# Tile-by-tile queries in the head of a two-layer decoder trunk, and the first expert choice in two groups of heads

## What is computed

```python
q = (hc @ w_query).reshape(T, PEER_HEADS, 2, PEER_DK)
s = jnp.einsum('thpd,phnd->thpn', q, sub_keys)
top_s, top_i = lax.top_k(s, K_SUB)
cand = top_s[:, :, 0, :, None] + top_s[:, :, 1, None, :]
best_s, best_c = lax.top_k(cand.reshape(T, PEER_HEADS, K_SUB * K_SUB), PEER_TOPK)
expert = i1 * N_KEYS + i2          # i1, i2: top_i at best_c
gate = softmax(best_s)
act = gelu(einsum('thkd,td->thk', u_tab[expert], hc))
x += einsum('thk,thkd->td', gate * act, v_tab[expert])
```

## Time and profile before

| | |
|---|---|
| runs | 3590.6, 3592.1, 3597.78 us; median 3592.1 |
| the profiled execution: span from its first to its last instruction | 3593.4 us (the page gives no other time of that execution) |
| PE busy | 2864.7 us, 80% |
| DVE busy | 2512.9 us, 70% |
| ACT busy | 1388.5 us, 39% |
| POOL busy | 1310.8 us, 36% |
| transfers | 1296.92 MB, mean 361 GB/s |
| mean granted TensorE clock | 0.900 |
| first expert row issued | at 463.60 us |

### The profile page before, as it was taken

The page is one execution under the profiler, slowest core; times in us unless marked ns, Lnnn a source line. Parts: engine busy times, 40 slices in busy tenths (PEclk is TensorE's granted clock), DMA queues, the critical chain, the costliest instruction groups (busy, mean ns, idle before and its releaser), DMA issues. The chain is left out here.

```text
span 3593.4 us, 28215 instructions
## 1 busy us (share of the span) xinstructions
PE 2864.7 (80%) x8084; PEld 1470.3 (41%) x8084; DVE 2512.9 (70%) x5180; ACT 1388.5 (39%) x3442; POOL 1310.8 (36%) x1033
## 2 busy tenths in 40 slices
PE   8899787778989778777988778878998786556556
PEld 4554635435436334433436334535445432112112
DVE  1411577787767979787667969787767977777775
ACT  2321225456433344456423344457433242223222
POOL 0000033345333344445433333345433334554552
PEclk9989898889999989889999989989999897778777
DMA  4224289899999999999999999899999999999996
GB/s 159 104 82 164 100 364 373 345 415 420 421 421 371 402 391 404 383 407 421 421 413 378 378 391 389 349 405 421 421 421 386 367 378 422 421 422 396 421 422 269
DMA packets 182971, 1296.92 MB, mean 361 GB/s; under 512 B 20384, under 2 KB 21920, under 8 KB 28192
## 3 DMA queue, kind: packets, MB, share of 16 engines
q0 software_dynamic: 147456, 1073.81, 72.8%
q1 hardware_dynamic: 35360, 221.31, 15.6%
HBM read 1292.94 MB, written 2.10 MB: 360 GB/s over the span
## 5 line engine op out<-in xcount | busy, mean ns | idle before, releaser
L590 POOL DMA_INDIRECT ring<-in_uv,experts x1024 | 1308.3, 1278 | 2235.9 <-DVE x L1310 928.6
L1434 PE MATMUL ps_sum<-ring,diag 128*128 128x512 f32 x2060 | 1172.7, 712 | 567.5 <-ACT diag L855 566.4
L1301 DVE SCALAR_TENSOR_TENSOR ring<-ring,h_ffn 128x1024 f32<-128x1024 f32 x1024 | 1236.1, 1220 | 298.3 <-DMA ring<-in_uv,experts 291.4
L1434 PEld LDWEIGHTS ps_sum<-ring,diag 128*128 128x128 f32 x2060 | 423.6, 220 | 1198.7 <-ACT diag L855 820.3
L1310 DVE SCALAR_TENSOR_TENSOR x<-ring,weight,x 128x1024 f32<-128x1024 f32 x509 | 652.6, 1282 | 164.0 <-ACT weight L859 163.7
L853 ACT ACTIVATE diag<-ident,dots 128x128 f32<-128x128 f32 x515 | 205.8, 400 | 725.1 <-DVE ring L1301 714.9
L857 ACT ACTIVATE dots<-dots 128x1 f32<-128x1 f32 x509 | 101.8, 200 | 686.0 <-DVE ring L1301 684.5
L1572 PE MATMUL ps_act<-area_h,wt 128*128 128x256 f32 x1536 | 348.3, 385 | 2.6 <-ACT area_h L606 2.6
L1700 PE MATMUL ps_act<-wt,area_h 128*128 128x512 f32 x768 | 338.3, 594 | 10.9 <-DMA wt<-in_weights 10.9
L1572 PEld LDWEIGHTS ps_act<-area_h,wt 128*128 128x128 f32 x1536 | 294.5, 193 | 61.4 <-issue 17.9
L1496 PE MATMUL ps_act<-wt,area_h 128*128 128x512 f32 (+1 forms) x704 | 306.3, 595 | 4.2 <-ACT area_h L606 4.2
(11 more groups left out here) (193 smaller groups left out, 2178.4 us busy)
## 6 DMA issues: line engine op xcount, KB each, us to landing
wt<-in_weights SPq DMA_DIRECT2D x182, 1024.0 KB, 9.1
ring<-in_uv,experts POOLq DMA_INDIRECT x1024, 13.4
wt<-in_weights SPq DMA_DIRECT2D x8, 832.0 KB, 9.0
wt<-in_weights SPq DMA_DIRECT2D x11, 512.0 KB, 8.2
wt<-in_weights SPq DMA_DIRECT2D x4, 768.0 KB, 8.8
x<-in_x SPq DMA_DIRECT2D x4, 512.0 KB, 5.2
area_y<-in_keys SPq DMA_DIRECT2D x4, 512.0 KB, 11.5
area_f<-in_keys SPq DMA_DIRECT2D x4, 512.0 KB, 14.9
```

The source lines that it names most:

```text
L590: pool.indirect_dma_start(ring[:, row.slot, :], None, a[f"uv{row.step // 2}"][:, :], bass.IndirectOffsetOnAxis(ap=experts[:, row.step % 2, ...
L1301: dve.scalar_tensor_tensor(u, u, 1.0, h_ffn[:, row.tile, :], ALU.mult, ALU.mult, accum_out=dots[:, row.j:row.j + 1]).then_inc(dots_ready, 1)
L1434: ins = pe.matmul(ps_sum[:, b, :], diag[:, row.pe_before % DIAGS, :], ring[:, row.slot, D + b * 512:D + (b + 1) * 512], start=row.pe_first ...
```

## The change

In the head, the queries are computed tile by tile. All eight query weight tiles are loaded into the eight slots of `ring`, which hold no rows yet, each with a semaphore of its own (`held`), and stay there for tile 1. `tile_query` computes one head for 128 tokens (`tile_scores` and `tile_rank` likewise). The choice of tile 0 is done in two groups of four heads (`topk_half`): the first group in the head, the second in step 0. GpSimd starts with row 0 when the first group's experts are there, and waits for the rest at row 64. Each of its first eight rows waits also until tile 1's query of that slot's head is through PE. The second group, the queries, scores and ranks of tile 1, and `x_norm` and `qkv` of step 1 are now stages of step 0, and the choice of tile 1 is spread between the stages of `x_norm` and the projection. The ffn row, the head's first gate and the scratch of the first choices lie in `area_kv` instead of `area_f`, `ring` and `area_y`. The diff shows ScalarE's `tile_scores` and PE's `tile_query`. Scores lie in `area_e` by head, all eight heads of one tile. Steps 1 to 3 keep their order. The four lines behind `TOPK_HALF_OPS` belong to `ROWS_IN`, `PE_PART`, `TICKS` and `ROWS_FIRST`.

```diff
+    "tile_query": (1, 0, 0, 0), "tile_scores": (1, 0, 0, 0), "tile_rank": (0, 0, 0, 10),
+TOPK_HALF_OPS = [3, 8, 8, 12, 4, 4, 4]
...
+    "tail_norm": 8, "tail_out": 6, "tile_query": 0, "tile_scores": 0, "tile_rank": 2.4, "topk_half": 1.6,
+           "out": 0, "query": 0.5, "scores": 0.5, "rank": 0.5, "topk": 1, "topk_half": 1, "taps": 1, "diff_sq": 1, "diff_norm": 1,
+         "out": 4, "query": 2, "tile_query": 2, "tail_out": 3}
+              "mla_qk", "mla_rope", "mix_turn", "rank", "tile_rank", "topk", "topk_half")
...
+    if stage[0] == "tile_rank" and stage[2] == 0:
+        return (0, 0, 0, 0, 0, 0, 0, 1)[stage[3]]
...
+def half_choice(g):
+    return [("topk_half", 0, 0, part, g) for part in range(len(TOPK_HALF_OPS))]
+
+def first_tile():
+    out = [("tile_query", 0, 0, 0)]
+    for i in range(1, 5):
+        out += [("tile_query", 0, 0, i), ("tile_scores", 0, 0, i - 1), ("tile_rank", 0, 0, i - 1)]
+    more = [[("tile_query", 0, 0, i), ("tile_scores", 0, 0, i - 1)] for i in range(5, HEADS)] + [[("tile_scores", 0, 0, HEADS - 1)]]
+    for i, part in enumerate(half_choice(0)):
+        out += [part] + (more[i] if i < len(more) else [])
+    return out
+
+def second_tile():
+    more = [[("tile_query", 0, 1, 0)]]
+    more += [[("tile_query", 0, 1, i), ("tile_scores", 0, 1, i - 1)] for i in range(1, HEADS)] + [[("tile_scores", 0, 1, HEADS - 1)]]
+    out = []
+    for st in [("tile_rank", 0, 0, i) for i in range(4, HEADS)] + half_choice(1):
+        out += [st] + (more.pop(0) if more else [])
+    return out + [("tile_rank", 0, 1, i) for i in range(HEADS)]
...
     if step == 0:
-        out += choice(0, 1)
+        out += second_tile()
...
-        for i in range(HEADS + 1):
+        for i in range(HEADS + 1 if d else 0):
...
-        out += choice(d, 0)
+        out += choice(d, 0) if d else first_tile()
...
-    if step < 1:
-        ahead = [("x_norm", 1)] + [("qkv", 1, n) for n in range(3)]
-        out = [st for st in out if st not in ahead]
-        if step < 0:
-            last = [st for st in out if st[0] == "topk"][-4:]
-            out = behind(out, [(("rank", 0, HEADS - 1), ahead[:1]), (last[0], ahead[1:2]), (last[3], ahead[2:])])
+    if step == 0:
+        ahead = [("x_norm", 1), ("qkv", 1, 0), ("qkv", 1, 1), ("diff_sq", 1), ("diff_norm", 1), ("qkv", 1, 2), ("diff_turn", 1, 0)]
+        second = choice(0, 1)
+        out = behind(out, [(("tile_rank", 0, 1, HEADS - 1), second[:1])] + [(place, [part]) for place, part in zip(ahead, second[1:])])
...
-                    load(0, NT_PLE + 4, DENSE_TILES[4:-HEADS])
+                    sp.dma_start(ffn_rows[0], a["ffn_rows"][0]).then_inc(row_loaded, 16)
+                    first = len(DENSE_TILES) - HEADS - 2 * HEADS
+                    load(0, NT_PLE + 4, DENSE_TILES[4:first])
+                    for i in range(HEADS):
+                        load(0, NT_PLE + first + 2 * i, DENSE_TILES[first + 2 * i:first + 2 * i + 2])
+                        sp.dma_start(ring[:, i, :], a["weights"][0, NT_PLE + NT_DENSE - HEADS + i, :, :]).then_inc(held[i], 16)
...
-                if row.j == 0:
+                if number == 0:
+                    pool.wait_ge(half_ready, 1)
+                elif row.j == 0 or number == ROWS // 2:
                     pool.wait_ge(experts_ready, row.tiles_before + 1)
-                if number >= RING:
+                if number < RING:
+                    pool.wait_ge(for_act, WHERE[("tile_query", 0, 1, number)].evacs + 1)
...
+            def tile_scores(at, d, t, i):
+                act.wait_ge(act_ops, at.act)
+                if t:
+                    act.wait_ge(dve_ops, WHERE[("tile_rank", d, 0, i)].dve + 10)
...
+            def tile_query(at, d, t, i):
+                hT_ready(WHERE[("tile_query", d, 0, 0)])
+                pe.wait_ge(held[i], 16)
+                w, b = ring[:, i, :].rearrange("p (k n) -> p k n", k=KT), act_bank()
+                for c in range(2):
+                    for k in range(KT):
+                        ins = pe.matmul(b[:, c * P:(c + 1) * P], w[:, k, c * P:(c + 1) * P], hT[:, k, t * P:(t + 1) * P],
+                                        start=(k == 0), stop=(k == KT - 1))
+                    if c:
+                        to_act(ins)
+                    tick()
```

More of the change, by code:

```diff
@@ L81, in counts @@
         return (0, part == len(TOPK_OPS) - 1, 0, TOPK_OPS[part])
+    if stage[0] == "topk_half":
+        part = stage[3]
+        return (0, part == len(TOPK_OPS) - 1, 0, TOPK_HALF_OPS[part])
     return COUNTS[stage[0]]
@@ L473, in trunk @@
         keys_loaded = sem("keys_loaded")
+        held = [sem(f"held{i}") for i in range(HEADS)]
         consts_made = sem("consts_made")
@@ L674, in x_norm @@
                     act.wait_ge(x_loaded[d], 16 * 2)
-                norm(at, d, "g_mix", ring[:, 1, 0:D] if d == 1 else squares[:, 0:D])
+                norm(at, d, "g_mix")
             def qkv(at, d, n):
@@ L840, in _ @@
                          branch_more=nothing, mix_turn=mix_turn,
-                         out=out, rows=nothing, tail_norm=tail_norm, tail_out=tail_out, ffn_norm=ffn_norm, query=query, scores=scores, rank=nothing, topk=topk, topk_late=topk)
+                         out=out, rows=nothing, tail_norm=tail_norm, tail_out=tail_out, ffn_norm=ffn_norm, query=query, scores=scores, rank=nothing, topk=topk, topk_late=topk,
+                         tile_query=tile_query, tile_scores=tile_scores, tile_rank=nothing, topk_half=topk)
             rows = Rows()
@@ L1193, in rank, with topk @@
                         link()
-            def topk(at, d, t, part):
-                sums = cand.rearrange("p (h i j) -> p h i j", h=HEADS, i=TOPK)
+            def topk(at, d, t, part, g=None):
+                hs = heads_in(g)
+                heads = range(hs.start, hs.stop)
+                n_heads, js = len(heads), slice(hs.start * TOPK, hs.stop * TOPK)
+                part_i, exps = part_is[d][:, :, js], exps_at[d][:, hs, :]
+                sums = cand.rearrange("p (h i j) -> p h i j", h=HEADS, i=TOPK)[:, hs, :, :]
                 lists = cand.rearrange("p (h c) -> p h c", h=HEADS)[:, :, 0:CANDS]
@@ L1213, in topk @@
+                    op(dve.scalar_tensor_tensor(top_f[:, hs, :, :].rearrange("p h c k -> p (h c) k"),
+                                                iota[:, :].unsqueeze(1).to_broadcast([P, 2 * n_heads, TOPK]), 128.0,
+                                                top_i[:, t, 2 * hs.start:2 * hs.stop, :], ALU.mult, ALU.add))
                 elif part == 1:
-                    for h in range(HEADS):
+                    for h in heads:
                         op(dve.max(best_v[:, h, 0:8], lists[:, h, :]))
@@ L1279, in _ @@
                          branch_first=branch, branch_more=branch,
-                         mix_turn=nothing, out=out, rows=nothing, tail_norm=tail_norm, tail_out=tail_out, ffn_norm=ffn_norm, query=nothing, scores=nothing, rank=rank, topk=topk, topk_late=topk)
+                         mix_turn=nothing, out=out, rows=nothing, tail_norm=tail_norm, tail_out=tail_out, ffn_norm=ffn_norm, query=nothing, scores=nothing, rank=rank, topk=topk, topk_late=topk,
+                         tile_query=nothing, tile_scores=nothing, tile_rank=tile_rank, topk_half=topk)
             rows = Rows()
@@ L1769, in _ @@
                          branch_more=branch, mix_turn=mix_turn,
-                         out=out, rows=nothing, tail_norm=tail_norm, tail_out=tail_out, ffn_norm=ffn_norm, query=query, scores=scores, rank=nothing, topk=nothing, topk_late=nothing)
+                         out=out, rows=nothing, tail_norm=tail_norm, tail_out=tail_out, ffn_norm=ffn_norm, query=query, scores=scores, rank=nothing, topk=nothing, topk_late=nothing,
+                         tile_query=tile_query, tile_scores=tile_scores, tile_rank=nothing, topk_half=nothing)
             pe.wait_ge(consts_loaded, 16 * N_CONSTS)
```

104 lines of the change are left out of this document (61 added, 43 removed).

## The result

The changed kernel takes 3614.07 us (median of 4 runs), the kernel before 3591.35 in the same comparison; the ratio is 1.0063, 95% interval 1.005 to 1.0077. The profiled execution spans 3609.9 us against 3593.4. The time lies above the stated range.

What follows compares the result with a forecast made beforehand. Row transfers at 421 GB/s were taken to bound all behind the head; 62.6 us earlier start less 5, 30 and 13 gave 14.6, taken as 15: 3577 us. Range 3552 to 3600, the forecast's own 3565 to 3587.

Steps and rivals of the forecast that it cites:

- Row 0 and the small matmuls: Head: 128-column query matmuls take 0.111 us each, so row 0 is issued at about 401 instead of 463.6, 62.6 us earlier.
- The slower rival: Head queries: small matmuls wait for their weights, 0.19 for 0.111 us, giving 3600 us or more; chance 0.14.
- The loop: First eight rows of step 0: PE alternates tile 1's queries with rows, 30 us newly empty, from 12 to 40.
- Fewer rows in the rest of the step: Later stages of step 0 get 0.948 instead of 1.158 rows a unit, 18% fewer; costs 13 us, 7 to 27.
- the gates: Gates of step 0: with 29 instead of 35 rows PE becomes the bound, and some 7 us open.
- all other stretches: Stretches of step 0 where transfers already pause keep their chains and lose rows: 6 us, between 0 and 20.
- The sum: Whole kernel: 62.6 - 5 - 30 - 13 = 14.6 us gained, taken as 15.
- the 5 us of weights: Start of step 0: two more of step 1's projection weight tiles fall behind the first row, costing 5 us.
- My check from step 2: Step 0 judged by step 2's 821.0 us: 836 to 851 us from row 0, a gain of 10 to 25.
- The engine-bound rival: PE's or VectorE's work sets step 0's length: gain -19 to +11, around 3592 us, no change; chance 0.17.

Runs made afterwards that it cites:

- thinner_before: The kernel before with 9.99 instead of 3 for each part of tile 1's choice in step 0 in the planner's table; 3628.9 us, 1.0099.
- groups_only: The kernel before with only tile 0's choice split in two groups of four heads, rows behind the first group; 3587.65 us, 0.9981.
- whole_choice_thicker: whole_choice_thick with 0.6 for a rank and 0.6 for a part of tile 1's choice, fewer rows ahead of the squares; 3570.35 us, 0.9938.
- whole_choice_thick: whole_choice_in_head with 1.2 for a rank, 1.5 for a part of tile 1's choice, and ScalarE's exponential moved earlier; 3558.39 us, 3562.63 in a second set.
- rows_behind_queries: The changed kernel with no row worked off before tile 1's last query, those rows given to tile 1's ranks; 3577.86 us, 0.9968.
- queries_first_thick: rows_behind_queries with fewer rows early: 1.2 instead of 3.5 for a rank, 1.5 instead of 3 for a part of tile 1's choice; 3590.3 us, 0.9996.
- share_shift: The kernel before with the running sum that deals rows to PE or VectorE started at 0.5 instead of 0.0; 3585.39 us, 0.9982.
- whole_choice_in_head: The changed kernel without the two groups: all of tile 0's choice in the head, tile 1's queries beside it on PE; 3577.45 us, 0.9967.
- thick_late: The changed kernel with fewer rows early in step 0: 1.0 for a rank of tile 1, 1.5 for a part of its choice; 3601.52 us, 1.0027.
- projection_behind: The kernel before with only the norm and projection of step 1 moved from the head into step 0; 3583.18 us, 0.9982.

## Why the prediction was wrong

1. **Row 0 and the small matmuls: right.** 402.27 for 401; a query of 128 columns takes 3.57 us, 0.112 us an instruction over runs of 32, for 0.111. The slower rival, whose place was here, fell. The Trainium skill (TensorE: Matmul & The Clock Gate, Back-to-back issue gap) gives 81 ns for a matmul of 128 columns in a stream of load and matmul pairs and 56 ns by itself; the factor of 1.45 estimated from that does not show in this trace: 0.112 us against 0.108, half of 0.216.

2. **The loop: right in mechanism, too small in size.** Rows 3 to 7 were forecast for 412, 424, 430, 437.5 and 451, and came at 413, 427, 434, 443 and 459. The term was 30 us newly empty; the first 60 us at 129 GB/s have 60 x (1 - 129/421) = 41.6 us of empty time, and the first 60 us before, at 412 GB/s, had 1.3. So 40 us are new, the upper bound of the term (12 to 40). Each row came 1 to 8 us later than I had put it.

3. **"Fewer rows in the rest of the step", 13 us with 7 to 27: this is the step that failed most.** Behind the first 60 us the step has 125.5 - 41.6 = 84 us of empty time, 48 before: 36 more, beyond the upper bound. The direction was right, the gates too (11 us for my 7). I had put 6 us on all other stretches. By their rates they opened by 7 us (squares to gates), 14 us (behind the gates) and 3 us (before the squares). My error was to look for stages that turn engine-bound in the gates alone. The reason shows in thinner_before, where one number of the table was changed: 22 rows less between squares and gate save 350.3 - 313.7 = 37 us of the 55 that their transfers take, six rows less in the gates save 1.5 of 15, and behind them 17 MB less (41 us at 421 GB/s) save 26.5 us. In the gates it is plain that PE sets the pace. For the other two stretches, where no engine is busy all the time, I take it that their own chains of waits are the longer there; no run shows which chain.

4. **The sum.** 61.3 - 5 - 40 - 36 = -20; `h_ffn` of step 1 starts 20.1 us later. This had to close, since empty time is counted as whatever part of the step's length the bytes at 421 GB/s do not fill. It shows how large the terms are, and what it checks is the 5 us of weights (361 x 880.3 against 395 x 798.8 is 2.3 MB more). My check from step 2 (836 to 851 us, measured 880.3) repeated the error: step 2 carries 1.10 rows a unit, not 0.95.

5. **The engine-bound rival** had a loss of 19 us at its end, near the result. Step 0 of the changed kernel has PE busy 60 us longer (726.7 for 666.6) and grew by 81. But two runs do not follow PE's sum: groups_only (18 us more work, 2.4 us more time) and whole_choice_thicker (5.5 us less work than whole_choice_thick, 10.8 us more time). The rival is unlikely by these and by the windows of thinner_before; it isn't excluded by a run made for it, since PE's share of the rows moved with every edit of the table.

Split by the experiments, step 0's 81.4 us of growth are 29.3 for the loop (removed in rows_behind_queries), 39.6 for a spread down to 0.948 (made in thinner_before, with PE's larger share of the rows), and 12.5 left, which has room for the 5 us of weights and for the 4.0 us between first rows; that rest was not tried by itself. The parts need not simply add. Left open: why the table's points do not lie in order (queries_first_thick slower than both of its neighbours, whole_choice_thicker slower than whole_choice_thick by 12 us). In share_shift another deal came with a step 0 that is 4 us shorter, and no run shows that the deal explains these.

## What to carry to other kernels

Where a background stream bounds the time and a plan interleaves it by shares, work moved behind its start can also dilute it everywhere later: compare the stream's units per stage with the ones that each stage can hide before counting the earlier start as gained, and set the shares anew (here 51 to 56 us lay between the changed kernel and its best rearrangement). And do not let an in-order engine serve consumers of a stream between the instructions that free the stream's first buffers: finish freeing first. Here that was worth 29 us of step 0 with the same start, and a start 21 us later (whole_choice_in_head) was still 37 us faster in all. An experiment on the spread must also hold fixed which engine takes the moved units; the ones here did not.

## What had not been expected of the hardware

The same head, instruction for instruction, ended up to 6 us earlier or later from kernel to kernel (row 0 at 397.0, 397.2, 399.2, 402.3 and 403.1 us in five kernels that share it). The order is that of the clock that TensorE was granted in the head: a mean of 0.95, 0.95, 0.94, 0.93 and 0.93. The same ten microseconds in the changed kernel and in thick_late, which come to this point of the head with the same instructions:

```profile
200.00:210.00 10.00, 8.57 (x36) 7.24 (x37) 0.33 (x2) 4.23 (x14) 0.00 (x0) 0.50 0.00 0
...
200.00:210.00 10.00, 9.31 (x27) 4.35 (x26) 1.39 (x2) 2.48 (x3) 0.00 (x0) 1.00 0.04 11
```

The changed kernel stays at the lower level (0.50, that is 1.2 GHz) here, while thick_late is already at 2.4 GHz. What made the clock rise earlier isn't shown. It goes beyond the head: in 18 runs of the kernel before on one chip the fastest (3582.2 us) had a mean clock of 0.904 and the slowest (3601.24) 0.898. Part of a difference of some microseconds between two kernels here can be the clock, and that holds for groups_only, projection_behind and share_shift above all.

Steps 1 and 2, which no experiment edited, lay between 799.8 and 812.8 and between 812.8 and 823.6 us in the profiles, in no order that follows the edits.
